# A decoder layer with a PEER mixer: activation stores issued by ScalarE right after the Gelu, the first loads of the down stage inside the up stage, and three pieces of ScalarE work in other places

## What is computed

```python
xn = rms_norm(x, norm1_g)
q, k, v, a, gt = split(xn @ w_in)               # 3*512 + 2*512 columns
attn = moba(rms_norm(q), rms_norm(k), v)        # block-sparse: own block of 256 keys and the top 3 past ones
conv = silu(rms_norm(causal_conv31(a * sigmoid(gt))))
h = x + concat(attn, conv) @ w_out
xn = rms_norm(h, norm2_g)
# PEER: 8 heads; scores of 128 + 128 product keys choose 16 of 128*128 experts
g, idx = softmax(top16(scores(xn @ w_query)))
act = gelu(xn . expert_u[idx])                   # expert_u, expert_v: 16384 x 1024
y = h + sum(g * act * expert_v[idx])
```

## Time and profile before

| | |
|---|---|
| median of 3 runs | 2017.74 us |
| profiled execution / its span | 2022.25 us / 2020.6 us |
| TensorE (PE) busy | 1909.5 us, 95% |
| VectorE (DVE) busy | 1390.6 us, 69% |
| GpSimd (POOL) busy | 1121.1 us, 55% |
| ScalarE (ACT) busy | 856.1 us, 42% |
| DMA moved | 508.8 MB, 252 GB/s over the span |

### The profile page before, as it was taken

One profiled execution on the slowest core, in us unless ns is written; L12 is line 12 of the kernel. 1 busy time (PEld: TensorE's weight loads), 2 busy tenths in 40 slices (PEclk: granted clock), 3 DMA queues, 4 the chain that ended last, 5 costly groups with the idle time before them and its releaser, 6 DMA issues.

```text
span 2020.6 us, 39020 instructions
## 1 busy us (share of the span) xinstructions
PE 1909.5 (95%) x14702; PEld 1812.4 (90%) x14702; DVE 1390.6 (69%) x2528; ACT 856.1 (42%) x1119; POOL 1121.1 (55%) x755
## 2 busy tenths in 40 slices
PE   6988988788999999999999999899979999999998
PEld 6977764357999999999999999899979999999998
DVE  3669665522589888954446775465537999999996
ACT  4233664422223455456665565344433333333332
POOL 3322222232235888876678888578854565656630
PEclk8999999799999999999999999899989999999999
DMA  4443878662124777777877989998978999999993
GB/s 157 85 108 132 289 251 285 220 246 84 63 84 152 229 222 229 230 214 236 290 259 247 336 314 345 338 327 312 344 251 298 338 361 343 354 357 343 353 330 114
DMA packets 253534, 508.80 MB, mean 252 GB/s; under 512 B 51041, under 2 KB 172962, under 8 KB 232642
## 3 DMA queue, kind: packets, MB, share of 16 engines
q1 hardware_dynamic: 202930, 369.56, 54.0%
q0 software_dynamic: 44032, 134.35, 18.4%
q10 hardware_dynamic: 6416, 2.78, 1.1%
HBM read 442.77 MB, written 63.73 MB: 251 GB/s over the span
## 4 chain that ended last, share of the span: by engine, by line
PE 78%; POOL 6%; DVE 5%; ACT 4%; DMA 3%; issue 2%; DVEq 1%; SPq 1%; ACTq 0%; POOLq 0%
PE pair L1548 22%; PE pair L1549 22%; PE pair L1550 22%; PE pair L1879 4%; PE pair L1693 3%; POOL w_lo L650 2%; POOL v_rows L661 2%; PE pair L1705 1%; DMA acts<-act_out 1%; POOL picked_a L654 1%; PE pair L1745 1%; PE pair L1831 1%; PE pair L1658 1%; PE pair L1558 1%; ACT page_kt L825 1%
## 5 line engine op out<-in xcount | busy, mean ns | idle before, releaser
L1548 PE MATMUL pair<-x_hi,w_hi 128*128 128x256 f32 (+2 forms) x2560 | 753.0, 294 | 34.9 <-DVE x_lo L1034 16.2
L1549 PE MATMUL pair<-x_lo,w_hi 128*128 128x256 f32 (+2 forms) x2560 | 742.5, 290 | 0.0
L1550 PE MATMUL pair<-x_hi,w_lo 128*128 128x256 f32 (+2 forms) x2560 | 740.6, 289 | 0.0
L1548 PEld LDWEIGHTS pair<-x_hi,w_hi 128*128 128x128 f32 x2560 | 487.0, 190 | 40.1 <-issue 26.1
L1549 PEld LDWEIGHTS pair<-x_lo,w_hi 128*128 128x128 f32 x2560 | 486.6, 190 | 0.2
L1550 PEld LDWEIGHTS pair<-x_hi,w_lo 128*128 128x128 f32 x2560 | 485.4, 190 | 0.0
L1548 PE MATMUL pair<-a_hi,w_hi 128*128 128x352 f32 x1024 | 333.3, 326 | 14.6 <-DVE w_lo L1487 13.8
L661 POOL DMA_INDIRECT v_rows<-in_v_t,at_row x192 | 200.0, 1042 | 250.6 <-DVE pair L1433 201.3
L1550 PE MATMUL pair<-a_hi,w_lo 128*128 128x352 f32 x1024 | 332.7, 325 | 0.0
L1549 PE MATMUL pair<-a_lo,w_hi 128*128 128x352 f32 x1024 | 332.2, 324 | 0.0
L650 POOL TENSOR_TENSOR w_lo<-w_raw,w_hi 128x1024 fp32r<-128x1024 f32 x116 | 275.9, 2403 | 87.0 <-ACT w_hi L918 86.9
(11 more groups left out here) (219 smaller groups left out, 2737.5 us busy)
## 6 DMA issues: line engine op xcount, KB each, us to landing
w_raw<-in_u_t SPq DMA_DIRECT2D x85, 1024.0 KB
v_raw<-in_u_t SPq DMA_DIRECT2D x43, 1024.0 KB
w_raw<-in_v_t SPq DMA_DIRECT2D x128, 256.0 KB
v_raw<-in_v_t SPq DMA_DIRECT2D x128, 256.0 KB
gates<-g_out SPq DMA_DIRECT2D x11, 2048.0 KB
g_in<-gates SPq DMA_DIRECT2D x16, 1408.0 KB
act<-acts SPq DMA_DIRECT2D x64, 352.0 KB
acts<-act_out SPq DMA_DIRECT2D x64, 288.0 KB
```

Of the source, the lines that this page charges most:

```text
L1548: te.matmul(out, s_hi, m_hi, start=start, stop=False)
L1549: te.matmul(out, s_hi, m_lo, start=False, stop=False)
L1550: return te.matmul(out, s_lo, m_hi, start=False, stop=stop)
```

## The change

Five edits. (1) The stores of activations are issued by ScalarE after `gelu_out(t, 1)` of the same pass, and no more by SyncE a pass later. (2) SyncE loads V's parts 0 to 2 in passes 125 to 127 in place of after the loop; in place of all at pass 93, activations 0 and gates of half 0 are loaded at 93, activations 1 at 94, gates of half 1 at 97. (3) In the first norm `high_w(0)` stands after the square of block 5 in place of after the root. (4) The sigmoids go from slot 15 to slot 20 and `finish_conv` from slots 17 to 20 to slots 22 to 25. (5) In the second norm the square stands ahead of `high_w` in odd blocks, and the last `high_w` stands after the root.

```diff
                     sp.dma_start(v_raw[part][:, WC // 4 * x:WC // 4 * (x + 1)].rearrange("p (j d) -> p j d", j=2),
                                  v_parts[quad, part, :, x]).then_inc(v_loaded[part], 16)
 
-            def store_acts(t):
-                slot = t % 2
-                sp.wait_ge(gelu_done, 2 * t + 2)
-                whole = acts[t % STEPS].rearrange("p (j n) -> p j n", j=2)
-                if t < STEPS:
-                    sp.dma_start(acts_sparse[t].rearrange("p (j n) -> p j n", j=2), act_out[:, slot, :, 0:NS])\
-                        .then_inc(acts_stored[slot], 16)
-                    sp.dma_start(whole[:, :, 0:FIRST - NS], act_out[:, slot, :, NS:FIRST]).then_inc(acts_stored[slot], 16)
-                else:
-                    sp.dma_start(whole[:, :, FIRST - NS:ND], act_out[:, slot, :, 0:N - FIRST])\
-                        .then_inc(acts_stored[slot], 16)
-
             by_tiles = gates.rearrange("c p (g i) t -> g p c (i t)", i=8)
 
             def load_acts(s, slot):
@@ -525,11 +513,11 @@
                 sp.wait_ge(w_split, W_CHUNKS - 2 + t)
                 load_u(t)
             for t in range(PASSES):
+                wait_low_u(sp, t)
                 if t + 3 < PASSES:
-                    wait_low_u(sp, t)
                     load_u(t + 3)
-                if t:
-                    store_acts(t - 1)
+                else:
+                    load_v(0, t + 3 - PASSES)
                 if t == TURN_AFTER[1]:
 
                     sp.wait_ge(rt_found, 2)
@@ -542,18 +530,16 @@
                 if t == LOADS_AT:
                     for parity in range(2):
                         sp.wait_ge(g_stored[parity], 16 * ((NG + 1 - parity) // 2))
-                    for half in range(2):
-                        load_gates(half, half)
+                for half in range(2):
+                    if t == LOADS_AT + half:
                         sp.wait_ge(acts_stored[half], stores_until(STEPS + half))
                         load_acts(half, half)
+                    if t == LOADS_AT + 4 * half:
+                        load_gates(half, half)
                 for first in range(2):
                     if t == PREPARE_AT[first] + 4:
                         sp.wait_ge(a_done, 2 * first + 2)
                         load_acts(first + 2, first)
-            for n in range(3):
-                wait_low_u(sp, PASSES - 3 + n)
-                load_v(0, n)
-            store_acts(PASSES - 1)
             for parity in range(2):
                 sp.wait_ge(acts_stored[parity], stores_until(PASSES - 2 + parity))
             load_v(0, 3)
@@ -691,13 +677,15 @@
 
         @block.scalar
         def _(sc):
-            def squares(dst, src, block_count, loaded, summed, done):
+            def squares(dst, src, block_count, loaded, summed, done, after=None):
 
                 for kd in range(block_count):
                     loaded(kd)
 
                     wait(sc, summed, kd - 1)
                     sc.activation(dst[:, kd % 2, :], src[:, kd, :], ACT.Square).then_inc(done, 1)
+                    if after is not None:
+                        after(kd)
 
             def root(banks, width, summed, count, done):
 
@@ -721,9 +709,9 @@
 
 
             sc.wait_ge(const_ready, 1)
-            squares(sq, resid, KD, lambda kd: sc.wait_ge(x_loaded[kd // 2], 16), sum1_done, sq1_done)
+            squares(sq, resid, KD, lambda kd: sc.wait_ge(x_loaded[kd // 2], 16), sum1_done, sq1_done,
+                    lambda kd: high_w(0) if kd == KD - 3 else None)
             root(pair[0], D, sum1_done, KD, root1_done)
-            high_w(0)
             high_x(scaled1, high1)
             high_w(1)
 
@@ -890,24 +878,25 @@
                 if at == 13:
                     root(pair[0], CH, sumc_done, CC, rootc_done)
                 if at == 15:
+                    keep_output(0)
+                    keep_probabilities(1)
+                if at == 20:
                     sc.wait_ge(z_done, 1)
                     for cc in range(CC):
                         sc.activation(sig_c[:, cc, :], conv[:, cc, :], ACT.Sigmoid).then_inc(sigc_done, 1)
-                    keep_output(0)
-                    keep_probabilities(1)
             keep_output(1)
 
             high_w(N_IN + 1)
 
 
-            def block_done(db):
-                sc.wait_ge(h_done, db + 1)
-
-                if db % 2:
+            def next_weights(db):
+
+                if db % 2 and db < KD - 1:
                     high_w(N_IN + db // 2 + 2)
 
-            squares(sq, resid, KD, block_done, sum2_done, sq2_done)
+            squares(sq, resid, KD, lambda db: sc.wait_ge(h_done, db + 1), sum2_done, sq2_done, next_weights)
             root(pair[2], D, sum2_done, KD, root2_done)
+            high_w(N_IN + N_OUT + 1)
             high_x(scaled2, high2)
 
 
@@ -931,6 +920,19 @@
 
                 width = FIRST if t < STEPS else N - FIRST
                 return bank(up_bank_of(t, j))[:, 0:width], act_out[:, t % 2, j, 0:width]
+
+            def store_acts(t):
+
+                slot = t % 2
+                sc.wait_ge(gelu_done, 2 * t + 2)
+                whole = acts[t % STEPS].rearrange("p (j n) -> p j n", j=2)
+                if t < STEPS:
+                    sc.dma_start(acts_sparse[t].rearrange("p (j n) -> p j n", j=2), act_out[:, slot, :, 0:NS])\
+                        .then_inc(acts_stored[slot], 16)
+                    sc.dma_start(whole[:, :, 0:FIRST - NS], act_out[:, slot, :, NS:FIRST]).then_inc(acts_stored[slot], 16)
+                else:
+                    sc.dma_start(whole[:, :, FIRST - NS:ND], act_out[:, slot, :, 0:N - FIRST])\
+                        .then_inc(acts_stored[slot], 16)
 
             def gelu_out(t, j):
 
@@ -977,6 +979,7 @@
                 for g in groups[1:3]:
                     keep_gates(g)
                 gelu_out(t, 1)
+                store_acts(t)
                 if t in EXP_AFTER:
                     nt = EXP_AFTER.index(t)
                     r = ROWS[nt]
@@ -1267,8 +1270,8 @@
                         last = v.scalar_tensor_tensor(conv[:, cc, :], conv[:, cc, :], conv_g[:, cc:cc + 1], rstd[:, :],
                                                       ALU.mult, ALU.mult)
                     last.then_inc(z_done, 1)
-                if 17 <= at < 17 + CC:
-                    finish_conv(at - 17)
+                if 22 <= at < 22 + CC:
+                    finish_conv(at - 22)
             mix_output(0)
             mix_output(1)
             v.memset(stats[:, 56:57], 0.0).then_inc(mix_ready, 1)
```

## The result

The changed kernel takes a median of 2035.51 us (6 runs, 2028.72 to 2040.40) against 2017.81 us before (6 runs, 2015.99 to 2021.14): ratio 1.0076, 95% interval 1.0063 to 1.0089, so 13 to 18 us **slower**. I had forecast 2017.0 and a range up to 2028.5. The profiled execution of after took 2033.14 us, with a span of 2031.5.

A forecast was written before the change was run, and what follows sets the result against it. TensorE, busy 95% of the span, was taken to bound the kernel. Terms -11.5 - 8.5 - 1.3 - 1.5 + 1.1 + 21.0 were summed to -0.8 us, giving 2017.0 us from 2017.74; range 2001 to 2028.5.

The forecast's parts named there:

- carry-over: Whole run: the profiled execution's 4.5 us above the median before was taken to hold after the change too.
- part 1: Stall at pass 95: store on ScalarE no longer waits behind SyncE's loads, saving idle and low clock: -11.5 us.
- part 6: Up stage: store issues on ScalarE delay U's high half past its slack: +21 us, bounds 0 and +43.
- part 2: Turn to the down stage: V's loads issued earlier, first chunk starts sooner: -8.5 us (-7 to -11).
- part 4: Sigmoids moved to slot 20: 3.5 us back at slot 15, 2.4 lost at slot 20; net -1.5 us.
- rival 3: Pass 95: stores still meet the DMA backlog, Gelu(95,0) waits as now, part 1 is 0: 2028.5 us; chance 0.10.
- plain passes: Some 34 of passes 3 to 46: every second one pays 0.47 us, +8.0 us within part 6.
- Exp passes: Five passes with an Exp, where U's high half is already late: +6.0 us within part 6.
- 3 us of low clock: Five Exp passes and the one after may lower TensorE's clock: +3 us (0 to +8) within part 6.
- rival 2: Passes 3 to 46: ScalarE's issues take longer than SyncE's, high half 1.8 us late: 2025.8 us; chance 0.20.
- Part 3: First norm: earlier high half frees GpSimd sooner, root 1.0 us later: -1.3 us (-2.4 to +1.0).
- Part 5: Second norm: root 1.6 us earlier, but GpSimd's low half holds VectorE's product: +1.1 us (-1.8 to +1.5).

The follow-up runs named there:

- e1: Kernel before with only the stores moved to ScalarE; loads, norms and sigmoids as before: 2036.64 us, ratio 1.0096.
- e2: Changed kernel with the stores back on SyncE, a pass later: 2009.46 us, ratio 0.9962 to the kernel before.
- e7: Kernel before with the reordered loads alone (gates, activations and V's first three parts): 2005.46 us, ratio 0.9931.
- e3: Changed kernel, but ScalarE issues the stores behind the copy of U's high half that follows: 2010.77 us, ratio 0.9962 to the kernel before.
- e5: Changed kernel, but below pass 64 ScalarE issues one store and SyncE the other: 2021.12 us, ratio 1.0007 to the kernel before.
- e6: Changed kernel, but below pass 64 the first store is split, so ScalarE issues three: 2054.84 us, ratio 1.0180 to the kernel before.
- e11: Kernel before with only V's first three parts loaded in passes 125 to 127: 2012.54 us, ratio 0.9976.
- e9: Kernel before with only the sigmoids at slot 20 and the convolution's end at slots 22 to 25: 2020.10 us, ratio 1.0024.
- e10: Changed kernel with the sigmoids back at slot 15 and the convolution's end at 17 to 20: 2032.20 us, ratio 1.0084 to the kernel before.

## Why the prediction was wrong

The median was missed by 18.5 us. 6.8 of these are the carry-over, and 11.7 are parts of the sum: 4.1 part 1, 2.4 part 6, 1.8 part 2, 1.5 part 4, and 1.9 small changes in stretches for which I had nothing. Part by part, by its own steps:

- **Part 1, the largest miss among the parts, and its mechanism failed.** -7.4 for -11.5. The stall of pass 95 went, but I had put it down to the store's place on SyncE's queue, and e1, e2 and e7 show otherwise. With the stores moved alone passes 90 to 99 gain 0.2 us, because U is late in the store's place (rival 3 in another form). With the loads spread alone they gain 8.4. I said that U has passes of lead; without the spread it had not. And the move itself costs 3.4 us in passes 92 to 94, where the store of pass 90 lands after 16.0 us.
- **Part 6, right in its mechanism and 2.4 low in its size.** +23.4 (19.0, 2.7 and 1.7) for +21.0. The delay (1.43 for 1.40 us) and the rhythm (every second plain pass) were right, and e3, e5 and e6 show that it is the place of the issue and a threshold. Its terms were off in both directions. The plain passes up to 46 cost 11.6 for 8.0: ten stops of 0.47 or 0.48 us and one of 0.78 cost 8.3 together, since a stop costs 0.26 more than its idle time, and the shorter waits in passes 24 to 27, 32 to 35, 40 and 41 cost 3.3. The Exp passes and those behind them cost 7.4 for 6.0. The 3 us of low clock didn't come (mean clock of passes 0 to 46: 1.00). At pass 46 to 64 the loss was 2.7 for 1.4, from 64 on 1.7 for 2.6. This is rival 2's side, but not its reason: ScalarE's issues took 0.52 and 0.64 us, as SyncE's do.
- **That 0.47 was forecast and found is luck.** By the rows shown the low half is ready 4.64 us after the Gelu, which leaves a slack of 5.70 - 4.64 = 1.06 and not 0.93, and an excess of 0.34. In the profile of after TensorE's next product was due not at the next Gelu but 5.53 us after the last (655.18 against 649.65) and started at 6.16, so 0.63 late. The brackets show 0.47 of this.
- **Part 2.** -6.7 for -8.5: the store of pass 127 took 5.8 us to the next load (1516.48 to 1522.29), 4.0 before. e11 gives the same turn by V's loads alone and e1 by the stores' alone: the two edits buy one gain.
- **Part 3** came out (-1.2 for -1.3), from two errors that offset each other: GpSimd's low half ended 4.0 us earlier and not 2.5 (20.12 for 24.08), and the root came 1.3 later and not 1.0. **Part 5** (+0.9 for +1.1) was right: the held product is in the trace.
- **Part 4, a step that failed.** I had one of two new waits, and took the load of V pages only for a limit to the gain. In the profile compared it is 0.0 for -1.5. Alone it costs 2.4 us in medians and 4.8 by the ratio (e9); e10 doesn't bear this out by the ratio. The other five profiles with the new place have an attention 2 to 8 us longer than after's, which may be why the median stands 2.4 above after's profiled execution; that isn't shown.
- **The carry-over, the largest single error.** I took it that a profiled execution stands as far above its median after as before. 4.4 above and 2.4 below make 6.8 of the 18.5 us. One execution of a kernel whose runs spread over 5 us before and 12 after tells little of where the next one stands.

Two slips in the sum are small: its terms give -0.7 and not -0.8, and part 5 has -1.8 and -1.6 for the same case.

Nearly all errors were to one side, where I had a balance of -23 and +22. Part 6 alone had a bound of +43, 22 above its centre, which makes 2039; the range ended at rival 3's centre, 2028.5, and took in nothing of it. The measured 2035.5 lies between the two.

By the ratios the stores alone are +19.4 us, the loads alone -13.9 and the sigmoids alone +4.8, which makes +10.3. Stores and loads each gain 6.6 to 7.7 us at the turn, which can be had only once, so that +17 to +18 would be expected and the ratio gives +15.3. With intervals of 3.4 to 4.4 us to either side of each term this fits, but it doesn't test the sigmoids' term.

**Still open:** what makes the attention up to 8 us longer in some executions with the new place of the sigmoids. The loads of V pages are issued later there; what their issue waited for wasn't followed. Nor is it known what the store of pass 90 stood behind.

## What to carry to other kernels

Look at what an issue of a DMA on a compute engine stands in front of. Here it cost ScalarE's time between two operations of the chain that feeds TensorE, and 0.3 us over passes 0 to 46 when it stood behind the start of a copy that had to run anyway. Count the slack of that chain first: with 0.76 us of delay the loss was 4.5 us, with 1.43 it was 19. A stop of a busy TensorE cost its idle time and 0.26 us besides, so many small stops are dearer than the table of waits says. If a stall stands behind a large load in a queue, move the large load: moving the small store only handed the wait to the next in line. And give a forecast that is a small balance of large terms a range as wide as the bounds of the largest.

## What was not expected of the hardware

- Two DMA issues on ScalarE cost 1.43 us of its time behind a Gelu, and none of it while a 1.91 us copy runs.
- Waits of 0.5 us every second pass, and single ones of 1.6, 2.0 and 2.6 us among them, left TensorE's granted clock at 1.00 over the whole of passes 0 to 46. The wait of 8.5 us before was followed by 0.53, and so was one of 2.01 us by 0.54 and in after one of 3.46 us, at 1007.38, by 0.50 over 3.4 us.
- A 1.4 MB gate load ahead of it made an activation load of 352 KB take 5.3 and 5.7 us (e1) and 7.1 and 6.4 us (before) to issue on SyncE. Where the loads are spread the activation loads take 0.4 to 0.7 us, but in e7 it is the load of U behind the gate load that takes 5.8 us to issue.
- A store on a queue of its own did not land sooner: that of pass 90 took 16.0 us issued by ScalarE (after) and 7.0 issued by SyncE (e7).
